# W2 block sums of a Strassen-like MLP computed on GpSimd instead of VectorE

## The chip, the cores and the metric

The kernel runs on one core of a Trainium2 chip. The metric is the device time of one execution in microseconds (us), as the median of several runs.

## What is computed

The reference is a two-layer streaming-encoder trunk on 512 frames of width 1024 in float32. Layer 0 mixes tokens by two gated linear recurrences, layer 1 by latent attention with rotary positions. Behind each mixer stands a squared-ReLU MLP of width 4096, and this case is about the MLPs:

```
def rope(x, cos, sin):
    ...
def sq_relu_mlp(h, w1, w2):
    return jnp.square(jax.nn.relu(h @ w1)) @ w2

def reference(x, positions, norm_gains, ..., mlp_w1, mlp_w2):
    for l in range(DEPTH):
        h = rmsnorm(x, norm_gains[l, 0])
        m = ...                                   # the layer's mixer
        x = x + rmsnorm(m, norm_gains[l, 1])
        h = rmsnorm(x, norm_gains[l, 2])
        x = x + rmsnorm(sq_relu_mlp(h, mlp_w1[l], mlp_w2[l]), norm_gains[l, 3])
    return x
```

## The kernel before

**Number format.** Each operand of a matrix product is split into a high and a low part, and three matmuls (`mm3`, L1827 to L1829: low by high, high by low, high by high) make one product. ScalarE casts the high part (`split_high`, L596 and L598; `operand`, L1072), then VectorE subtracts to get the low part (`split_low`, L605 without and L607 with a gain; `operand_low`, L1535). TensorE waits for the low part by the count `lo_ready` or `block_low`.

**The MLP.** The hidden width of 4096 is walked through in slices of 512. Six of them (SUBS = 6) are multiplied with W2 by a Winograd-Strassen scheme of seven products of half size instead of eight. For each slice s the scheme needs four blocks of W2 as they are (B11, B12, B21, B22, each 256 rows by 512 columns, held as 128 partitions by 1024 elements) and four sums of them, made in place in the buffers of the raw blocks: T1 = B12 - B11 in the buffer of B11, T2 = B22 - T1 in the buffer `spare`, T4 = B21 - T2 in the buffer of B21, T3 = B22 - B12 in the buffer of B12. Likewise four sums of blocks of the hidden values (S1 to S4). The raw blocks lie in `raw`. `spare` also holds, at another time of the step, the third of the four units of W1 (called w1_2 here; w1_0, w1_1 and w1_3 lie in `stage`). The four w1 units serve the up projection.

**One step.** `body(b)` is a step, b = 1 to 6 in each layer; steps 2 to 5 are one loop. Every engine has its own list in program order, and the lists meet in semaphores only. On TensorE a step is: up tile 0 (24 matmuls, w1_3 is needed at the 19th), products P1, P2, P1, P2 (first and second half of the tokens, six matmuls each), up tile 1, P5, P3, P5, P3, up tile 2, P7, P4, P7, up tile 3, P6, P4, P6. P5 uses T1, P7 uses T3, P4 uses T4 and P6 uses T2. Two banks of PSUM serve the up tiles and the products P1, P5, P7 and P6 in turn, so that a product or tile waits until the bank was read: up tiles by ScalarE (`up`, relu at L1064, square at L1066), products by VectorE (`gather`, L1550 in the first step and L1554 in the others). The second P1 waits for the relu of up tile 0, and that relu waits until VectorE has split S2, since it overwrites the buffer of S2. The second P5 waits for the relu of up tile 1, which stands in ScalarE's list behind the high parts of T1, T3 and T4.

**VectorE's list** in a step begins with the split of B21, the sum S4 (`hid_sum`, L1539) and the split of S2; then the four sums T1, T2, T4, T3 (`weight_sum`, L1543) stand between two gathers and the splits of T1, S4 and T3. At the step's end come the splits of B11, S3, w1_0 and w1_1, a gather, w1_2, the sums S1 and S2, and the splits of A12 and w1_3, all for the next step.

**GpSimd's list** has the pairwise differences of the gates (L788) in layer 0's mixer, later the rope angles (L807 to L819, a chain in which each instruction waits for the one before), a load of a gain, and four memsets for the attention mask (to L828). Behind them stand only DMA issues until the end.

**The DMA queue of SyncE** (`load_mlp`) loads the raw blocks of the next step: B11 when T1 was split (L704 and L681), B22 when the fourth sum is there, B12 when T3 was split, B21 when T4 was split, w1_3 when w1_0 was split.

The sums in VectorE's list, word for word:

```
weight_sum("T1", "B12", "B11", (stage_in[RAW_OF["B12"]], b12_loaded[layer, s] + 16 * i))
gather("P1", 0, 1, 1, s, i)
weight_sum("T2", "B22", "T1", (t_ready, made + 1))
gather("P1", 1, 0, 3, s, i)
low("T1", s, i)
weight_sum("T4", "B21", "T2", (t_ready, made + 2))
operand_low("S4", s, i)
weight_sum("T3", "B22", "B12", (t_ready, made + 3))
low("T3", s, i)
```

## Time and profile before

| what | value |
|---|---|
| median of 3 runs | 1232.18 us (1231.8 to 1235.79) |
| the profiled execution, its own time | 1229.68 us |
| its span in the profile | 1228.0 us |
| TensorE busy | 1174.5 us, 96% |
| VectorE busy | 816.6 us, 67% |
| ScalarE busy | 627.1 us, 51% |
| GpSimd busy | 114.6 us, 9% |
| mean granted clock of TensorE | 0.987 |

The profile is of one execution, and its time lies 2.5 us under the median. Its own time is 1.7 us more than its span, which is what lies before the first and behind the last instruction. PE is TensorE (PEld its weight loads), DVE is VectorE, ACT is ScalarE, POOL is GpSimd. Matmuls are pipelined: one of 512 columns is shown with 0.39 us, but the next begins 0.227 us behind it. Likewise a VectorE instruction's end overlaps the start of the next by about 0.08 us.

### The profile page before, as it was taken

The page shows a single profiled execution, that of the slowest core. Times are in us where ns is not written, and L with a number is a line of the kernel's source. Part 1 is how long each engine was busy: PE and PEld are TensorE (multiplying, and loading weights), DVE is VectorE, ACT ScalarE, POOL GpSimd, SP SyncE. Part 2 cuts the span into 40 slices and gives each one's busy share as a digit, 9 for nine tenths or more (in the row PEclk, how much of TensorE's full clock was granted, in tenths as well). Part 3 has the DMA queues.
Part 4 walks back from the last instruction along what each step waited for, and adds up shares of the span by engine and source line. Part 5 has one row for each costly group of instructions (what it writes and reads, how often), then busy time and mean ns, then how long its engine had stood idle before and what let it go on. Part 6 is the DMA issues. An engine that isn't in the chain of part 4 may idle for free.

```text
span 1228.0 us, 16266 instructions
## 1 busy us (share of the span) xinstructions
PE 1174.5 (96%) x5851; PEld 968.3 (79%) x5851; DVE 816.6 (67%) x1216; ACT 627.1 (51%) x1177; POOL 114.6 (9%) x129
## 2 busy tenths in 40 slices
PE   6999999999989999999899998999999999999897
PEld 5777788877968888888778776778978888888686
DVE  5566867875587687668556256865577677767644
ACT  5554555454645454545435675654655445545331
POOL 2331212310191000000000000100000000000000
PEclk9999899999999999999999999999999999999999
DMA  4322121133423332231222232212423332331221
GB/s 143 102 69 68 40 66 53 52 112 130 146 68 105 119 110 94 89 117 52 86 86 84 63 88 59 65 40 86 155 88 101 103 120 89 99 105 49 69 86 68
DMA packets 87490, 108.18 MB, mean 88 GB/s; under 512 B 9186, under 2 KB 48195, under 8 KB 87428
## 3 DMA queue, kind: packets, MB, share of 16 engines
q1 hardware_dynamic: 85684, 101.85, 26.1%
q0 software_dynamic: 1744, 5.51, 1.4%
q8 instruction: 38, 0.62, 0.2%
q14 instruction: 24, 0.20, 0.0%
HBM read 104.20 MB, written 2.10 MB: 87 GB/s over the span
## 4 chain that ended last, share of the span: by engine, by line
PE 79%; DVE 10%; ACT 7%; issue 2%; DMA 1%; POOL 0%; DVEq 0%; SPq 0%; ACTq 0%
PE bank L1827 21%; PE bank L1829 20%; PE bank L1828 20%; PE pp L1827 3%; PE pp L1828 3%; PE pp L1829 3%; PE pp L1969 2%; PE po L2308 1%; DVE y L1630 1%; DVE w_lo L607 1%; PE pp L1872 1%; DMA stage<-in_mlp_w 1%; ACT w_hi L598 1%; ACT w_hi L596 1%; PE pp L2289 1%
## 5 line engine op out<-in xcount | busy, mean ns | idle before, releaser
L1827 PE MATMUL bank<-h_lo,w_hi 128*128 128x512 f32 (+4 forms) x764 | 293.3, 384 | 12.0 <-DVE w_lo L607 5.9
L1829 PE MATMUL bank<-h_hi,w_hi 128*128 128x512 f32 (+4 forms) x764 | 289.8, 379 | 0.0
L1828 PE MATMUL bank<-h_hi,w_lo 128*128 128x512 f32 (+4 forms) x764 | 289.7, 379 | 0.0
L1827 PEld LDWEIGHTS bank<-h_lo,w_hi 128*128 128x128 f32 (+1 forms) x764 | 142.5, 187 | 43.3 <-DVE w_lo L607 7.5
L1829 PEld LDWEIGHTS bank<-h_hi,w_hi 128*128 128x128 f32 (+1 forms) x764 | 142.6, 187 | 27.3
L1828 PEld LDWEIGHTS bank<-h_hi,w_lo 128*128 128x128 f32 (+1 forms) x764 | 142.7, 187 | 25.4
L1827 PE MATMUL bank<-wx,a_hl 128*128 128x512 f32 x320 | 125.9, 393 | 0.5 <-ACT sq L1064 0.5
L1828 PE MATMUL bank<-wx,a_hl 128*128 128x512 f32 x320 | 125.0, 391 | 0.0
L1829 PE MATMUL bank<-wx,a_hl 128*128 128x512 f32 x320 | 125.0, 391 | 0.0
L596 ACT CAST wx<-raw 128x1024 fp32r<-128x1024 f32 x72 | 74.5, 1048 | 98.2 <-DVE raw L1543 67.0
L1554 DVE TENSOR_TENSOR y<-y,bank 128x512 f32<-128x512 f32 x80 | 54.8, 684 | 88.2 <-PE bank L1829 88.2
L605 DVE TENSOR_TENSOR wx<-raw,wx 128x1024 fp32r<-128x1024 f32 x72 | 88.7, 1232 | 30.0 <-ACT wx L596 29.7
L607 DVE SCALAR_TENSOR_TENSOR w_lo<-stage,vec,w_hi 128x512 fp32r<-128x512 f32 (+2 forms) x128 | 82.7, 697 | 21.0 <-ACT w_hi L598 21.0
L598 ACT ACTIVATE w_hi<-stage,vec 128x512 fp32r<-128x512 f32 (+2 forms) x128 | 78.4, 668 | 16.3 <-DMA stage<-in_mlp_w 15.8
L788 POOL TENSOR_TENSOR dec<-b_sb 128x512 f32<-128x512 f32 x48 | 58.1, 1222 | 185.3 <-DVE b_sb L1419 70.8
L605 DVE TENSOR_TENSOR w_lo<-stage,w_hi 128x1024 fp32r<-128x1024 f32 (+1 forms) x45 | 57.3, 1274 | 24.0 <-ACT w_hi L596 12.2
L1827 PEld LDWEIGHTS bank<-wx,a_hl 128*128 128x128 f32 x320 | 60.4, 189 | 13.2 <-ACT sq L1064 0.9
L1829 PEld LDWEIGHTS bank<-wx,a_hl 128*128 128x128 f32 x320 | 60.3, 189 | 12.7
L1828 PEld LDWEIGHTS bank<-wx,a_hl 128*128 128x128 f32 x320 | 60.4, 189 | 12.2
L596 ACT CAST w_hi<-stage 128x1024 fp32r<-128x1024 f32 (+1 forms) x45 | 46.0, 1025 | 11.5 <-DMA stage<-in_mlp_w 8.5
L1064 ACT ACTIVATE tmp<-bank 128x512 f32<-128x512 f32 x28 | 16.7, 598 | 65.5 <-PE bank L1829 65.3
L1827 PE MATMUL bank<-w_lo,a_hl 128*128 128x512 f32 x112 | 45.4, 406 | 3.0 <-DVE a_hl L1432 1.6
(362 smaller groups left out, 2175.6 us busy)
## 6 DMA issues: line engine op xcount, KB each, us to landing
stage<-in_mlp_w SPq DMA_DIRECT2D x68, 512.0 KB, 3.7
raw<-in_mlp_w SPq DMA_DIRECT2D x48, 512.0 KB, 3.5
stage<-in_ev_w_in SPq DMA_DIRECT2D x28, 512.0 KB, 3.8
spare<-in_mlp_w SPq DMA_DIRECT2D x12, 512.0 KB, 4.8
stage<-in_ev_w_out SPq DMA_DIRECT2D x8, 512.0 KB, 3.5
stage<-in_od_w_out SPq DMA_DIRECT2D x8, 512.0 KB, 3.5
stage<-in_od_w_in SPq DMA_DIRECT2D x10, 256.0 KB, 2.9
x_tok<-in_x SPq DMA_DIRECT2D x4, 512.0 KB, 5.3
```

What stands on the lines that cost most here:

```text
L596: ins = nc.scalar.copy(hi, src)
L598: ins = nc.scalar.activation(hi, src, ACT.Copy, scale=vec[:, g:g + 1])
L605: ins = nc.vector.tensor_tensor(lo, src, hi.bitcast(F32), ALU.subtract)
L607: ins = nc.vector.scalar_tensor_tensor(out=lo, in0=src, scalar=vec[:, g:g + 1], in1=hi.bitcast(F32), op0=ALU.mult, op1=ALU.subtract)
L788: nc.gpsimd.tensor_tensor(dec[:, item % 3, :].rearrange("p (b j) -> p b j", j=2 * L), b_sb[:, :].rearrange("p (b j) -> p b j", j=2 * L), r ...
L1064: nc.scalar.activation(f, banks[m][:, :], ACT.Relu).then_inc(up_read, 1)
L1554: nc.vector.tensor_tensor(dst, dst, banks[src][:, :], ALU.add).then_inc(prod_read, 1)
L1630: nc.vector.tensor_tensor(dst, a, b, ALU.add).then_inc(c_ready, 1)
L1827: nc.tensor.matmul(dst, wh, xl_, start=first, stop=False)
L1828: nc.tensor.matmul(dst, wl, xh, start=False, stop=False)
L1829: return nc.tensor.matmul(dst, wh, xh, start=False, stop=last)
L1969: ins = nc.tensor.matmul(dst[o], k_, q_, start=True, stop=True)
```

## The change

The four sums per step leave VectorE's list and stand in GpSimd's. Those of layer 0 stand behind the rope angles and the mask's memsets, those of layer 1 at the end of the list. GpSimd waits by name for what VectorE's order gave for free: T1 for the split of B11 and the load of B12, T2 for the split of w1_2 (whose buffer it overwrites), T4 for the split of B21. The order T1, T2, T4, T3 stays. The load of the next B11 now also waits for T2, which reads T1 out of that buffer.

```diff
@@ load_mlp, on SyncE
                     t_split("T1", 0, i)
+                    sp.wait_ge(t_ready, SUM_N * layer + 2 + 4 * i)
                     load_block("B11", 1, i)
@@ on GpSimd
+            def weight_sums(layer):
+                block_at = {b: buffers[RAW_OF[b]] for b in RAW_OF}
+
+                def weight_sum(what, a, b, after):
+                    pool.wait_ge(*after)
+                    nc.gpsimd.tensor_tensor(block_at[what], block_at[a], block_at[b], ALU.subtract).then_inc(t_ready, 1)
+
+                def is_split(u):
+                    pool.wait_ge(hi_ready, u + 1)
+                    pool.wait_ge(lo_ready, u + 1)
+
+                for sub in range(SUBS):
+                    made = SUM_N * layer + 4 * sub
+                    is_split(unit_no[("B11", layer, sub)])
+                    weight_sum("T1", "B12", "B11", (stage_in[RAW_OF["B12"]], b12_loaded[layer, sub]))
+                    is_split(unit_no[("w1", layer, sub + 1, 2)])
+                    weight_sum("T2", "B22", "T1", (t_ready, made + 1))
+                    is_split(unit_no[("B21", layer, sub)])
+                    weight_sum("T4", "B21", "T2", (t_ready, made + 2))
+                    weight_sum("T3", "B22", "B12", (t_ready, made + 3))
...
             nc.gpsimd.memset(mask_q[0:1, 0:P // 2].bitcast(F32), MASKED).then_inc(consts_ready, 1)
             nc.gpsimd.memset(mask_k[0:1, P // 2:P].bitcast(F32), 1.0).then_inc(consts_ready, 1)
+            weight_sums(0)
             pool.wait_ge(x_new[1], KD)
             load_gain(2)
...
             pool.wait_ge(x_new[2], KD)
             load_gain(3)
+            weight_sums(1)
@@ body of mlp, on VectorE
-                    weight_sum("T1", "B12", "B11", (stage_in[RAW_OF["B12"]], b12_loaded[layer, s] + 16 * i))
                     gather("P1", 0, 1, 1, s, i)
-                    weight_sum("T2", "B22", "T1", (t_ready, made + 1))
                     gather("P1", 1, 0, 3, s, i)
                     low("T1", s, i)
-                    weight_sum("T4", "B21", "T2", (t_ready, made + 2))
                     operand_low("S4", s, i)
-                    weight_sum("T3", "B22", "B12", (t_ready, made + 3))
                     low("T3", s, i)
```

VectorE's list in the first step of layer 0, before (here `wx<-raw,wx` are the splits of B21, T1 and T3, `tmp<-tmp,sq` is the sum S4, `a_hl<-sq,a_hl` the split of S2, `a_hl<-tmp,a_hl` that of S4, `y<-bank` a gather):

```order
L605 TENSOR_TENSOR wx<-raw,wx 128x1024 [waits hi_ready]
L1539 TENSOR_TENSOR tmp<-tmp,sq 128x2x256 [waits s_ready]
L1535 TENSOR_TENSOR a_hl<-sq,a_hl 128x512 [waits block_high]
L1543 TENSOR_TENSOR raw<-raw 128x1024 [waits stage_in3]
L1550 COPY y<-bank 128x512 [waits prod_done]
L1543 TENSOR_TENSOR spare<-raw 128x1024 [waits t_ready]
L1550 COPY y<-bank 128x512 [waits prod_done]
L605 TENSOR_TENSOR wx<-raw,wx 128x1024 [waits hi_ready]
L1543 TENSOR_TENSOR raw<-raw,spare 128x1024 [waits t_ready]
L1535 TENSOR_TENSOR a_hl<-tmp,a_hl 128x512 [waits block_high]
L1543 TENSOR_TENSOR raw<-raw 128x1024 [waits t_ready]
L605 TENSOR_TENSOR wx<-raw,wx 128x1024 [waits hi_ready]
```

Without the four rows of L1543 the list reads as below; nothing else of it has moved, and the lines' numbers are 22 higher because of the function added above them:

```order
L605 TENSOR_TENSOR wx<-raw,wx 128x1024 [waits hi_ready]
L1561 TENSOR_TENSOR tmp<-tmp,sq 128x2x256 [waits s_ready]
L1557 TENSOR_TENSOR a_hl<-sq,a_hl 128x512 [waits block_high]
L1567 COPY y<-bank 128x512 [waits prod_done] x2
L605 TENSOR_TENSOR wx<-raw,wx 128x1024 [waits hi_ready]
L1557 TENSOR_TENSOR a_hl<-tmp,a_hl 128x512 [waits block_high]
L605 TENSOR_TENSOR wx<-raw,wx 128x1024 [waits hi_ready]
```

GpSimd's list of the changed kernel, from the end of the rope angles into the first step's sums of layer 0 (L802 is the sum; T1, T2, T4, T3 in this order):

```order
L841 TENSOR_SCALAR cosd<-cosd 128x512 [waits pool_chain]
L795 DMA gbc<-in_norm_gains 128x1024 [waits sin_arg]
L847 MEMSET mask_q 128x128
L848 MEMSET mask_k 128x128 [waits pool_chain]
L849 MEMSET mask_q 1x64 [waits pool_chain]
L850 MEMSET mask_k 1x64
L802 TENSOR_TENSOR raw<-raw 128x1024 [waits stage_in3,lo_ready,hi_ready]
L802 TENSOR_TENSOR spare<-raw 128x1024 [waits t_ready,lo_ready,hi_ready]
L802 TENSOR_TENSOR raw<-raw,spare 128x1024 [waits t_ready,lo_ready,hi_ready]
L802 TENSOR_TENSOR raw<-raw 128x1024 [waits t_ready]
```

The sums now stand behind the whole angle chain, and a sum no longer waits for its place in VectorE's list: from the second step on it starts as soon as the named splits are done, T1 and T2 already at the end of the step before.

## Rows read from the trace of the kernel before

**Rows 1.** Busy time by stretch; columns: stretch, us, PE, PEld, DVE, ACT, POOL, PEclk, DMA.

```profile
440.00:480.00 40.00, 40.00 (x178) 33.14 (x177) 29.21 (x38) 20.81 (x30) 0.00 (x0) 1.00 0.31 104
...
356.00:360.00 4.00, 4.00 (x12) 3.10 (x12) 4.00 (x5) 0.14 (x1) 3.83 (x3) 0.59 0.72 251
```

**Rows 2.** Waits of TensorE over the whole span: total us, times, longest.

```profile
PE bank L1827 <- DVE tmp L1665: 12.0, 2, 6.0
```

**Rows 3.** The sums, line L1543: count, ns min/median/max, first and last start.

```profile
L1543 DVE TENSOR_TENSOR raw<-raw x24: 1212/1217/2304, 359.4 to 1119.8; 128x1024 f32<-128x1024 f32 x24
```

**Rows 4.** Time line, GpSimd, rope angles: start us, us, instruction.

```profile
342.09 1.30 POOL L817 TENSOR_TENSOR sind<-rinv,gbc 128x512 f32<-128x512 f32 x1
343.48 1.49 POOL L816 TENSOR_SCALAR gbc<-gbc 128x512 f32<-128x512 f32 x1
...
359.31 1.32 POOL L817 TENSOR_TENSOR cosd<-rinv,gbc 128x512 f32<-128x512 f32 x1
360.72 2.35 POOL L816 TENSOR_SCALAR gbc<-gbc 128x512 f32<-128x512 f32 x1
...
372.58 0.14 POOL L828 MEMSET mask_k<- 1x64 f32 x1
```

**Rows 5.** The same of VectorE beside them, first step of layer 0.

```profile
359.41 2.30 DVE L1543 TENSOR_TENSOR raw<-raw 128x1024 f32<-128x1024 f32 x1
...
367.15 1.80 DVE L1535 TENSOR_TENSOR a_hl<-tmp,a_hl 128x512 fp32r<-128x512 f32 x1
```

**Rows 6.** Line L788, two-input differences on GpSimd: count, ns min/median/max.

```profile
L788 POOL TENSOR_TENSOR dec<-b_sb x48: 1037/1154/2067, 43.6 to 251.5; 128x512 f32<-128x512 f32 x48
```

**Rows 7.** Time line of VectorE around the start of layer 0's second step.

```profile
386.80 1.23 DVE L605 TENSOR_TENSOR wx<-raw,wx 128x1024 fp32r<-128x1024 f32 x1 [0.39 <-ACT wx L596]
387.94 0.68 DVE L1535 TENSOR_TENSOR a_hl<-rinv,a_hl 128x512 fp32r<-128x512 f32 x1
388.56 2.74 DVE L607 SCALAR_TENSOR_TENSOR w_lo<-stage,vec,w_hi 128x512 fp32r<-128x512 f32 x4
392.51 0.69 DVE L1550 COPY y<-bank 128x512 f32<-128x512 f32 x1 [1.22 <-PE bank L1829]
393.12 1.41 DVE L607 SCALAR_TENSOR_TENSOR w_lo<-spare,vec,w_hi 128x512 fp32r<-128x512 f32 x2
394.44 0.68 DVE L1539 TENSOR_TENSOR sq<-sq,tmp 128x512 f32<-128x512 f32 x1
...
396.37 1.41 DVE L607 SCALAR_TENSOR_TENSOR w_lo<-stage,vec,w_hi 128x512 fp32r<-128x512 f32 x2
...
398.90 1.22 DVE L605 TENSOR_TENSOR wx<-raw,wx 128x1024 fp32r<-128x1024 f32 x1
...
400.64 0.68 DVE L1535 TENSOR_TENSOR a_hl<-sq,a_hl 128x512 fp32r<-128x512 f32 x1
...
423.88 0.69 DVE L1554 TENSOR_TENSOR y<-y,bank 128x512 f32<-128x512 f32 x1 [4.07 <-PE bank L1829]
```

**Rows 8.** Time line of TensorE: two places of a second step, three of first steps.

```profile
399.11 0.39 PE L1827 MATMUL bank<-h_lo,w_hi 128*128 128x512 f32 x1
...
403.19 0.39 PE L1827 MATMUL bank<-wx,a_hl 128*128 128x512 f32 x1
...
355.78 0.50 PE L1827 MATMUL bank<-h_lo,w_hi 128*128 128x512 f32 x1 [2.65 <-DVE w_lo L607]
...
373.14 0.50 PE L1827 MATMUL bank<-wx,a_hl 128*128 128x512 f32 x1 [0.51 <-ACT sq L1064]
...
906.55 0.50 PE L1827 MATMUL bank<-h_lo,w_hi 128*128 128x512 f32 x1 [2.17 <-DVE w_lo L607]
```

**Rows 9.** Time line of ScalarE: high parts of T3 and T4, and a relu.

```profile
370.60 2.00 ACT L596 CAST wx<-raw 128x1024 fp32r<-128x1024 f32 x2 [7.28 <-DVE raw L1543]
...
401.41 0.60 ACT L1064 ACTIVATE sq<-bank 128x512 f32<-128x512 f32 x1 [3.91 <-DVE a_hl L1535]
```

**Rows 10.** VectorE in layer 1's first step, ahead of the split of w1_3.

```profile
904.48 0.69 DVE L1535 TENSOR_TENSOR a_hl<-tmp,a_hl 128x512 fp32r<-128x512 f32 x1 [1.39 <-ACT a_hl L1072]
```

More of the change, by code:

```diff
@@ L1526, in mlp @@
                 banks = [bank[(n0 + m) % 2] for m in range(4)]
-                flat_block = {b: buffers[RAW_OF[b]] for b in RAW_OF}
                 def low(what, sub, i):
@@ L1539, in hid_sum @@
                     nc.vector.tensor_tensor(hid_block[what], hid_block[a], hid_block[b], op).then_inc(s_ready, 1)
-                def weight_sum(what, a, b, after):
-                    dve.wait_ge(*after)
-                    nc.vector.tensor_tensor(flat_block[what], flat_block[a], flat_block[b],
-                                            ALU.subtract).then_inc(t_ready, 1)
                 def gather(product, tt, src, count, s, i):
```

## The prediction

> **What bounds the kernel now.** I read the page's first part, then the busy time by stretch, then TensorE's waits, and last the time lines of one step. The first shows TensorE busy for 96% of the span and VectorE for 67% (the table of the profile before). The stretches say more: in a middle step TensorE is busy for all 40 of 40 us at the full clock, and VectorE for 29.2 [rows 1]. A step is 180 matmuls at 0.227 us, 40.8 us, and nothing but TensorE sets it. So the 4.6 us that four sums take from VectorE in a step (4 of 1.14 us from start to start; 1.217 us each by the median of their line [rows 3]) lie beside TensorE's work already. A gain could come only where TensorE waits for VectorE because of a sum. The largest such wait, twice 6.0 us at L1665 behind the last step of each MLP [rows 2], comes behind steps in which VectorE idles anyway (4.07 us ahead of one gather in every step [rows 7]), so a relief inside the step does not reach it. What is left is the question what the sums cost when GpSimd makes them.
>
> **What one sum costs on GpSimd.** The trace has no such instruction of 1024 elements. A two-input instruction of 512 elements takes 1.30 us while VectorE is idle [rows 4], and 1.15 us by the median of L788, where one input repeats one element [rows 6]. Twice 1.30 is 2.6, twice 1.04 (the shortest of L788) is 2.1; something like 0.15 us is spent once per instruction (a memset of 64 elements takes 0.14 [rows 4]), so I take 2.45 us, nearest to the row that has two true inputs, and keep 2.1 and 2.6 as ends. On VectorE it was 1.22.
>
> The Trainium skill (GPSIMD Engine Reference, Performance versus the Vector engine) gives 4497 ns for a two-input add of 2048 elements; half of that is 2.25 us, and by it the sum below would be some 6 us smaller.
>
> **What the two engines do to each other.** At 359.31 GpSimd starts a two-input instruction that ends at 360.63. VectorE's first sum starts 0.10 us later and takes 2.30 us instead of 1.22: it stands still until GpSimd is through and then takes its usual time [rows 4, 5]. The same at 367.15, 1.80 us for a split that takes 0.68 elsewhere [rows 5, 7]. And at 360.72 GpSimd takes 2.35 us for what it does in 1.49 with VectorE idle [rows 4]: it waits until the sum that runs is finished, but it is served before VectorE's next one. So one of the two engines holds something for a whole instruction when VectorE has two SBUF inputs, and they alternate. I put the hold of a 1024-element sum at 2.4 us.
>
> The Trainium skill (SBUF — State Buffer, Who interferes with whom) speaks against the change with the same picture: a port pair shared by the two engines, an exclusive lock, and the second one to issue blocks fully. If that page were wrong and these rows had another cause, the first rival below would hold.
>
> **The middle steps: walk through the one that begins at 395.03.** Every instruction of VectorE here except the gathers has two SBUF inputs.
> - The split of B11 (386.80) frees T1 on GpSimd at 388.0. VectorE is then splitting S3 (387.94) [rows 7]. T1 gets its turn at 388.55 and holds until 390.95. The four w1 pieces that began at 388.56 begin at 390.95, and w1_1 is done at 393.6 instead of 391.2. The idle 1.22 us ahead of the gather at 392.51 [rows 7] take up half of it: gather from 393.6, w1_2 until 395.55.
> - The split of w1_2 frees T2. VectorE runs S1 (before at 394.44 [rows 7], now 395.55 to 396.2), T2 holds 396.2 to 398.6. Then S2 and the split of A12 (0.6 us each) and w1_3 (two of 0.67), done at 401.15 where it was 397.7. TensorE needs it at 399.11 [rows 8]. **First stall 2.1 us.**
> - Behind that come a gather, the split of S1, the split of B21 (before at 398.90 [rows 7]) until 403.5, and S4. The split of B21 frees T4, which holds 404.1 to 406.5. The split of S2 (before at 400.64 [rows 7]) ends at 407.1, the relu of up tile 0 waits for just that (as it did at 401.41 [rows 9]) and ends at 407.8, and the second P1 waits for the relu. It began at 403.19 [rows 8]; with the first stall it would at 405.3. **Second stall 2.5 us.**
> - T3 holds 2.4 us while VectorE has two gathers; their banks are needed only by up tile 1, at 405.9 before and 410.5 now. Cost nothing. T1, T3, T4 and T2 are then there before they were, and their splits have the idle 4.07 us of [rows 7] behind them. B11, B22, B12 and B21 are loaded behind those splits with more than 15 us before use, and the new wait for T2 is long fulfilled when T1 is split. Cost nothing. The load of w1_3 comes 2.4 us later behind w1_0 and its cast too, but VectorE reaches its split later still.
>
> That is 4.6 us a step; with h for the hold it is about 3h - 2.6. Each MLP has five such steps (2 to 6): 10 x 4.6 = 46 us.
>
> **Layer 1, first step.** T1 finds VectorE idle. T2 holds 2.4 us behind S1, and 1.39 us of idleness stood there ahead of the split of A12 [rows 10]; TensorE already waits 2.17 us for w1_3 [rows 8], so the first stall grows by 0.9 at once. T4 comes as in the other steps and costs 2.0. **2.9 us.**
>
> **Layer 0, first step.** Here the sums stand behind the angles, and those end with the memset at 372.58 [rows 4], when T3 had already been made. Without four sums beside it GpSimd loses some 2 us less to VectorE (0.86 us at 360.72 alone [rows 4]), so T1 runs 370.8 to 373.2, T2 to 375.7. VectorE splits T1 behind T2 (until 376.8), T4 holds until 379.2, S4's split until 379.8, T3 until 382.3. ScalarE casts T3 and T4 in 2.0 us as before [rows 9], and the relu of up tile 1 ends at 384.9. The second P5 waits for it, and began at 373.14 [rows 8]. **11.8 us.** TensorE stands still for 7 us of these; a stretch near half clock followed the stall of 2.65 us at 355.78 [rows 8] (12 matmuls in 4 us and a granted clock of 0.59 from 356 to 360 [rows 1]), six matmuls lost, 1.4 us. I add one such: **1.4 us.** GpSimd's later work (gain loads, rotary halves) waits for x or for VectorE, not for its own list: nothing.
>
> **The sum.** 46 + 2.9 + 11.8 + 1.4 = 62 us. The profiled execution took 1229.7, so 1292 by it; it lies 2.5 us under the median of the runs, and on that I predict 1294. The hold between 2.05 and 2.6 us moves ten steps by -1.0 and +0.6 each: 1283 to 1301.
>
> **Rivals.**
> - *The port costs VectorE nothing.* If VectorE's instructions go first and GpSimd takes the gaps, the middle steps stay at 40.8 us, because all four sums are needed 10 us or more later. Left are 11.8 + 1.4: **1245**. Against it stand the two stretched rows [rows 5]; for it, that no 1024-element sum on GpSimd has been seen. 12%.
> - *Only one stall per step.* If T4's wait for the split ends over 0.6 us late, the split of S2 goes ahead of T4, and the second stall is gone: 62 - 11 x 2.3 gives **1269**. GpSimd would need 0.6 us to notice a semaphore. 10%.
> - *The clock falls in every step.* Two stalls of over 2 us stand within 9 us, and the one of 2.65 us at 355.78 was followed by a stretch near half clock [rows 1, 8]. With 1.4 us for each of 11 steps: **1309**. Against it: the stall of 2.17 us at 906.55 [rows 8] was followed by none. 10%.
> - *Faster.* If VectorE carries a backlog from the sums of step 6 into the chain at L1665, TensorE's 12.0 us of waits there [rows 2] shrink by up to four sums per layer, 2 x 4.6 us: **1223**, provided that GpSimd's hold costs nothing and the angles are done in time. It decides only if VectorE has no idle time behind T3; it has 4.07 us and more in each step [rows 7]. 2%.
> - *No change.* The sums' lateness in layer 0's first step would have to vanish too, for instance if the angle chain without VectorE's sums beside it ended 9 us earlier. 2%.
>
> **How the numbers follow.** Forecast 64%. The predicted time is the forecast's. 1260 to 1311 holds it, the single stall and the clock case: 84%. The first rival lies outside. A measurement of this kernel can tell some 0.3% (4 us) from no change: faster 2%, within 0.3% 2%, slower 96%.
>
> **What the profile of the changed kernel would show.** Right: 48 sums on POOL of about 2.4 us; TensorE under 37 of 40 us in a middle step, with stalls behind the split of w1_3 (VectorE, L607) and behind the relu (ScalarE) before the second P1; VectorE splits of 512 elements that take some 3 us; a gap near 370 in layer 0 that ends with ScalarE's relu near 385. Wrong: middle steps of 40.8 us, or sums on POOL that are stretched themselves to 3 us and more while VectorE's are not.

## The result and the profile after

| | before | after |
|---|---|---|
| median of 3 runs | 1232.18 us (1231.8 to 1235.79) | 1264.21 us (1263.87 to 1266.02) |
| the profiled execution, its own time | 1229.68 us | 1266.02 us |
| its span | 1228.0 us | 1264.3 us |
| TensorE busy | 1174.5 us, 96% | 1186.7 us, 94% |
| VectorE busy | 816.6 us, 67% | 822.0 us, 65% |
| GpSimd busy | 114.6 us, 9% | 245.7 us, 19% |
| mean granted clock | 0.987 | 0.982 |

The ratio is 1.0258, with a 95% interval of 1.0231 to 1.0285: 32 us slower. The forecast was 1294 us, 62 us slower. The direction and the range held, but the likeliest case did not: half of the loss it names is not there. The time is near that of the rival "only one stall per step" (1269).

VectorE gave 48 sums of 1.2 us away, some 58 us, and yet its busy time rose by 5 us. What it had saved is in its record again as time in which it stood still behind GpSimd. Busy time by stretch, the same 40 us as in [rows 1] (columns as there), and the 4 us behind layer 1's first stall:

```profile
440.00:480.00 40.00, 38.52 (x170) 31.38 (x169) 29.94 (x33) 19.44 (x29) 11.21 (x4) 1.00 0.32 105
```

```profile
932.00:936.00 4.00, 4.00 (x12) 3.11 (x11) 2.58 (x4) 1.30 (x3) 2.49 (x1) 0.57 0.75 260
```

TensorE was busy for 40.00 of 40 us there; now it is for 38.52, where the forecast wanted less than 37. The four sums are GpSimd's 11.21 us. The sums by form (count, ns min/median/max, first and last start), in place of [rows 3]:

```profile
L802 POOL TENSOR_TENSOR raw<-raw x24: 2336/2402/2747, 368.1 to 1152.4; 128x1024 f32<-128x1024 f32 x24
L802 POOL TENSOR_TENSOR spare<-raw x12: 2348/2732/2740, 370.6 to 1141.3; 128x1024 f32<-128x1024 f32 x12
L802 POOL TENSOR_TENSOR raw<-raw,spare x12: 3134/3336/3358, 373.1 to 1149.0; 128x1024 f32<-128x1024 f32 x12
```

A sum that does not have to wait takes 2.34 to 2.40 us (T3, in the first row; so do the first two of layer 0). T1 and T2 show 2.73, and T4, in the third row, 3.34. What is above 2.4 is taken as waiting for VectorE: 0.35 us for T1 and T2, 0.94 for T4. The forecast expected stretched rows on VectorE alone, and had named sums of 3 us and more as a sign that it was wrong. T4's 0.94 us is the first sign of what it had wrong.

TensorE's waits, as in [rows 2] (total us, times, longest):

```profile
PE bank L1840 <- DVE w_lo L607: 21.9, 14, 3.1
PE bank L1840 <- DVE tmp L1678: 12.0, 2, 6.0
```

The wait for w1_3 (VectorE's `w_lo`) was 5.9 us in 3 places and is now 21.9 us in 14. The wait of 12.0 us behind the last step of each MLP is what it was. The steps themselves, from up tile 0 to the next up tile 0: a middle step took 40.80 us and takes 42.72, in both layers.

| part of the span | before | after | difference |
|---|---|---|---|
| start to up tile 1 of layer 0's first step | 364.31 | 362.92 | -1.4 |
| from there to up tile 0 of the second step | 30.72 | 42.23 | +11.5 |
| from there to up tile 1 of layer 0's sixth step | 174.08 | 183.83 | +9.8 |
| from there to up tile 1 of layer 1's first step | 344.38 | 351.28 | +6.9 |
| from there to up tile 1 of layer 1's sixth step | 203.99 | 213.38 | +9.4 |
| from there to the end of the span | 110.5 | 110.6 | +0.2 |

The fourth row is not the change's alone: the same stretch took from 344.4 to 350.9 us in the executions profiled for this study whose steps were undisturbed. Of its 6.9 us, 4.7 lie ahead of the first matmul of layer 1's MLP and 2.2 between that and up tile 1 of its first step. The medians differ by 32 us, the two profiled executions by 36.

**One middle step, on VectorE, GpSimd, ScalarE and TensorE.** It is the step of [rows 7]; everything lies later by 10 us because of the first step. VectorE (start us, us, instruction):

```profile
398.67 4.88 DVE L607 SCALAR_TENSOR_TENSOR w_lo<-stage,vec,w_hi 128x512 fp32r<-128x512 f32 x4
...
406.11 2.79 DVE L1561 TENSOR_TENSOR sq<-sq 128x512 f32<-128x512 f32 x1
408.82 0.68 DVE L1557 TENSOR_TENSOR a_hl<-tmp,a_hl 128x512 fp32r<-128x512 f32 x1
409.43 1.40 DVE L607 SCALAR_TENSOR_TENSOR w_lo<-stage,vec,w_hi 128x512 fp32r<-128x512 f32 x2
410.75 0.68 DVE L1567 COPY y<-bank 128x512 f32<-128x512 f32 x1
...
411.95 1.21 DVE L605 TENSOR_TENSOR wx<-raw,wx 128x1024 fp32r<-128x1024 f32 x1
413.09 0.68 DVE L1561 TENSOR_TENSOR tmp<-tmp,sq 128x512 f32<-128x512 f32 x1
413.69 0.68 DVE L1557 TENSOR_TENSOR a_hl<-sq,a_hl 128x512 fp32r<-128x512 f32 x1
414.29 0.67 DVE L1571 TENSOR_TENSOR y<-y,bank 128x512 f32<-128x512 f32 x1
```

GpSimd, the four sums T1, T2, T4, T3:

```profile
398.27 2.74 POOL L802 TENSOR_TENSOR raw<-raw 128x1024 f32<-128x1024 f32 x1 [19.28 <-DVE wx L605]
405.61 2.74 POOL L802 TENSOR_TENSOR spare<-raw 128x1024 f32<-128x1024 f32 x1 [4.59 <-DVE w_lo L607]
413.30 3.34 POOL L802 TENSOR_TENSOR raw<-raw,spare 128x1024 f32<-128x1024 f32 x1 [4.95 <-DVE wx L605]
416.71 2.39 POOL L802 TENSOR_TENSOR raw<-raw 128x1024 f32<-128x1024 f32 x1
```

ScalarE's relu of up tile 0:

```profile
414.46 0.60 ACT L1088 ACTIVATE sq<-bank 128x512 f32<-128x512 f32 x1 [4.71 <-DVE a_hl L1557]
```

TensorE, the matmul that needs w1_3 and the first of the second P1:

```profile
410.88 0.50 PE L1840 MATMUL bank<-h_lo,w_hi 128*128 128x512 f32 x1 [1.49 <-DVE w_lo L607]
...
415.13 0.47 PE L1840 MATMUL bank<-wx,a_hl 128*128 128x512 f32 x1
```

T1 holds back the four w1 pieces (4.88 us instead of 2.74) and T2 the sum S2 (2.79 instead of 0.69). With that w1_3 is split late, and TensorE's matmul at 410.88 starts 1.88 us behind the one before it (409.00), where 0.23 is usual. That is 1.65 us; slower starts of the matmuls behind the wait make up the rest of the 1.92 that the step has lost. That is the forecast's first stall. Then T4 asks at 413.30, while S4 is being summed. The forecast let it in next, ahead of the split of S2. It was not: the split of S2 follows S4 at once (413.69, 0.68 us), T4 gets its turn only behind it, the relu comes at 414.46, and the second P1 begins without a stall, though with nothing to spare: the relu ends at 415.06, and the matmul starts at 415.13. VectorE's gather at 414.29 takes its usual 0.67 us beside T4: one of its operands lies in PSUM.

**Layer 0's first step.** GpSimd, from the end of the angle chain on (in place of the last row of [rows 4]):

```profile
367.95 0.14 POOL L850 MEMSET mask_k<- 1x64 f32 x1
368.06 2.34 POOL L802 TENSOR_TENSOR raw<-raw 128x1024 f32<-128x1024 f32 x1
370.57 2.35 POOL L802 TENSOR_TENSOR spare<-raw 128x1024 f32<-128x1024 f32 x1 [0.17 <-POOL raw L802]
373.08 3.13 POOL L802 TENSOR_TENSOR raw<-raw,spare 128x1024 f32<-128x1024 f32 x1 [0.17 <-POOL spare L802]
376.30 2.70 POOL L802 TENSOR_TENSOR raw<-raw 128x1024 f32<-128x1024 f32 x1
```

VectorE beside it, the splits of T1 and S4 (the second was 1.80 us in [rows 5]):

```profile
371.51 2.49 DVE L605 TENSOR_TENSOR wx<-raw,wx 128x1024 fp32r<-128x1024 f32 x1 [9.05 <-ACT wx L596]
373.92 2.85 DVE L1557 TENSOR_TENSOR a_hl<-tmp,a_hl 128x512 fp32r<-128x512 f32 x1
```

ScalarE, in place of [rows 9], and TensorE behind both of its stalls:

```profile
379.08 1.99 ACT L596 CAST wx<-raw 128x1024 fp32r<-128x1024 f32 x2 [7.09 <-POOL raw L802]
380.98 0.59 ACT L1088 ACTIVATE sq<-bank 128x512 f32<-128x512 f32 x1
```

```profile
374.10 0.77 PE L1840 MATMUL bank<-wx,a_hl 128*128 128x512 f32 x1 [5.57 <-issue]
...
381.62 0.50 PE L1840 MATMUL bank<-wx,a_hl 128*128 128x512 f32 x1 [1.88 <-ACT sq L1088]
```

Here the forecast held nearly row for row: T1 and T2, the split of T1 behind T2, T4 ahead of the split of S4, T3, two casts, relu, second P5. Only the angle chain ended 4.6 us earlier than before (2 us were expected; 1.4 us of the 4.6 is that the whole step began earlier in this execution), and the larger stall, of 5.6 us, sits ahead of the first P5, which needs the split T1.

### The profile page after: what moved, and what is told of

Same layout as the page of the kernel before. It is cut to its first block, busy times and chain, and to the rows that moved or that the text cites. A ratio compares the mean times of both kernels' runs of the same rounds, so it can differ in the third digit from the quotient of the medians.

```text
span 1264.3 us, 16278 instructions
## 1 busy us (share of the span) xinstructions
PE 1186.7 (94%) x5851; PEld 970.9 (77%) x5851; DVE 822.0 (65%) x1168; ACT 627.8 (50%) x1177; POOL 245.7 (19%) x177
## 4 chain that ended last, share of the span: by engine, by line
PE 64%; DVE 15%; ACT 8%; issue 7%; POOL 4%; DMA 2%; DVEq 0%; SPq 0%; ACTq 0%; POOLq 0%
PE bank L1840 17%; PE bank L1841 16%; PE bank L1842 16%; DVE w_lo L607 4%; PE pp L1841 2%; PE pp L1842 2%; PE pp L1840 2%; PE po L2321 1%; DVE y L1643 1%; PE pp L1982 1%; ACT wx L596 1%; DVE sq L1561 1%; PE pp L1885 1%; DVE a_hl L1557 1%; DMA stage<-in_mlp_w 1%
## 5 line engine op out<-in xcount | busy, mean ns | idle before, releaser
L1840 PE MATMUL bank<-h_lo,w_hi 128*128 128x512 f32 (+4 forms) x764 | 295.3, 387 | 27.8 <-DVE w_lo L607 21.9
L1840 PEld LDWEIGHTS bank<-h_lo,w_hi 128*128 128x128 f32 (+1 forms) x764 | 143.0, 187 | 63.0 <-DVE w_lo L607 27.8
L1840 PE MATMUL bank<-wx,a_hl 128*128 128x512 f32 x320 | 128.1, 400 | 9.0 <-issue 5.6
L1842 PE MATMUL bank<-wx,a_hl 128*128 128x512 f32 x320 | 126.1, 394 | 0.0
L1841 PE MATMUL bank<-wx,a_hl 128*128 128x512 f32 x320 | 126.1, 394 | 0.0
L605 DVE TENSOR_TENSOR wx<-raw,wx 128x1024 fp32r<-128x1024 f32 x72 | 104.6, 1452 | 28.4 <-ACT wx L596 28.1
L607 DVE SCALAR_TENSOR_TENSOR w_lo<-stage,vec,w_hi 128x512 fp32r<-128x512 f32 (+2 forms) x128 | 104.5, 866 | 19.3 <-ACT w_hi L598 19.3
L802 POOL TENSOR_TENSOR raw<-raw 128x1024 f32<-128x1024 f32 x24 | 61.2, 2549 | 230.7 <-DVE wx L605 229.7
L1088 ACT ACTIVATE sq<-bank 128x512 f32<-128x512 f32 x28 | 16.7, 598 | 90.2 <-DVE a_hl L1557 55.0
L596 ACT CAST w_hi<-stage 128x1024 fp32r<-128x1024 f32 (+1 forms) x45 | 46.0, 1024 | 11.9 <-DMA stage<-in_mlp_w 8.6
```

The lines of the kernel that those rows point to most:

```text
L596: ins = nc.scalar.copy(hi, src)
L605: ins = nc.vector.tensor_tensor(lo, src, hi.bitcast(F32), ALU.subtract)
L607: ins = nc.vector.scalar_tensor_tensor(out=lo, in0=src, scalar=vec[:, g:g + 1], in1=hi.bitcast(F32), op0=ALU.mult, op1=ALU.subtract)
L802: nc.gpsimd.tensor_tensor(block_at[what], block_at[a], block_at[b], ALU.subtract).then_inc(t_ready, 1)
L1088: nc.scalar.activation(f, banks[m][:, :], ACT.Relu).then_inc(up_read, 1)
L1840: nc.tensor.matmul(dst, wh, xl_, start=first, stop=False)
```

## The experiments

Three questions were open: does each part of the loss come from where the time lines put it, what decides whether T4 goes ahead of the split of S2, and does any placement of the sums on GpSimd beat the kernel before. Kernels are named by what is edited. Where a kernel was run once only, its time is compared with the median of the kernel before on the same chip, and the reading rests on its time lines. Ratios and their 95% intervals are worked out from all runs of a comparison and can differ a little from the quotient of the two medians.

**1. Layer 0's sums on VectorE as before (T2, T4 and T3 at their old places too), layer 1's on GpSimd.**

```diff
             nc.gpsimd.memset(mask_k[0:1, P // 2:P].bitcast(F32), 1.0).then_inc(consts_ready, 1)
-            weight_sums(0)
...
+                    on_dve = layer == 0
+                    if on_dve:
+                        weight_sum("T1", "B12", "B11", (stage_in[RAW_OF["B12"]], b12_loaded[layer, s] + 16 * i))
...
```

> Layer 0's sums back on VectorE, layer 1's on GpSimd as in the change. Theory P (a port that one engine holds for a whole instruction): layer 1 pays 1.9 us in each of its five middle steps and some 2 in its first, so about 1243 to 1245 us, and its steps last 42.7 us while those of layer 0 last 40.8. Rival L (the cost is mostly lateness behind the rope angles in layer 0): about 1234, steps of 40.8 in both layers.

Measured: 1241.44 us, ratio 1.0101 (1.0074 to 1.0128), 12.4 us over the 1229.07 of the kernel before. Middle steps take 40.80 us in layer 0 and 42.7 in layer 1. The loss per step belongs to the steps whose sums GpSimd makes, and layer 0 carries the rest, some 20 us.

**2. T4 asked for a little earlier.** GpSimd waits for the low part of a block only, one semaphore instead of two.

```diff
                 def is_split(u):
-                    pool.wait_ge(hi_ready, u + 1)
                     pool.wait_ge(lo_ready, u + 1)
```

> GpSimd waits for lo_ready alone ahead of T1, T2 and T4, not for hi_ready and lo_ready, so that each sum is asked for a little earlier (the low part implies the high one). T4 then comes earlier into VectorE's sum S4. If the split of S2 went ahead of T4 by a close race in time, T4 now goes first, the second P1 stalls by some 2.4 us, a middle step lasts about 45 us and the time is near 1288. If the order does not hang on the moment of asking, steps stay at 42.7 us and the time at 1264.

Measured: 1260.56 us, ratio 1.0256 (1.0228 to 1.0284), as the change itself. T4 stood at GpSimd 0.44 us before the split of S2 began instead of 0.39, took 3.39 us, and still came behind it. 0.05 us decide nothing; the edit moves the moment by no more.

**3. T1 asked for only behind the split of S2.** One wait more, so that all four sums stand where VectorE has gathers to do and TensorE has its P1 and P2.

```diff
                     is_split(unit_no[("B11", layer, sub)])
+                    pool.wait_ge(block_low["S2"], SUBS * layer + sub + 1)
                     weight_sum("T1", "B12", "B11", (stage_in[RAW_OF["B12"]], b12_loaded[layer, sub]))
```

> T1 on GpSimd also waits until VectorE has split S2, so that no sum runs beside the splits of w1 at the end of a step. Theory P: the stall ahead of w1_3 is gone, middle steps last 40.8 us, and only layer 0's first step stays late: about 1243 us. Rival W (the stall has another cause, such as the later load of w1_3 or more DMA traffic): middle steps stay near 42.7 us and the time near 1264.

Measured: 1260.12 us, ratio 1.0259 (1.0230 to 1.0288). Neither side had it. The stall at w1_3 is gone from every middle step (10.88 us from up tile 0 to up tile 1, as before), so the hold by T1 and T2 was its cause. But a new wait took its place: the four sums now follow each other, and ScalarE casts T3 and T4 ahead of the relu of up tile 1, for which the second P5 waits. GpSimd, ScalarE and TensorE in one middle step:

```profile
464.93 2.72 POOL L802 TENSOR_TENSOR raw<-raw 128x1024 f32<-128x1024 f32 x1
```

```profile
467.74 2.00 ACT L596 CAST wx<-raw 128x1024 fp32r<-128x1024 f32 x2 [7.19 <-POOL raw L802]
469.64 0.59 ACT L1089 ACTIVATE sq<-bank 128x512 f32<-128x512 f32 x1
```

```profile
470.28 0.50 PE L1841 MATMUL bank<-wx,a_hl 128*128 128x512 f32 x1 [1.14 <-ACT sq L1089]
```

T3 is there at 467.65, the casts end at 469.74, and the second P5 begins 1.3 us late: 42.24 us a step.

**4. The wait of 3, and the sums of layer 0's first step ahead of the rope angles.**

```diff
+            weight_sums(0, range(1))
             ch.link(nc.gpsimd.tensor_copy(angle, pos_i))
...
-            weight_sums(0)
+            weight_sums(0, range(1, SUBS))
```

> As e3, and the four sums of layer 0's first step stand ahead of the rope angles. Theory P: no stall by sums anywhere; and since the angles no longer run beside the first step's splits of w1, TensorE's stalls of 1.0 and 2.7 us and the stretch at half clock there go too: about 1227 to 1230 us, 2 to 5 less than before the change. Rival: the angles, now some 30 us later, hold VectorE up in the second step instead, and T1 of the second step comes late behind them: 1236 or more.

Measured: 1249.95 us, ratio 1.0171 (1.0144 to 1.0199). The first step is clean, 30.27 us where the change has 42.23. But the angles, put off by four sums, run into the second step beside its own sums and VectorE's w1 splits, and that step takes 49.5 us (four stalls of 1.1 to 2.7 us); the others take 42.24. Work of some 33 us on GpSimd that shares something with VectorE costs wherever it meets a step: moved from one, it costs in the next.

**5. The wait of 3, and ScalarE's relu of up tile 1 ahead of the casts of T3 and T4.** VectorE's split of T3 moves behind that of A22 to match.

```diff
@@ body of mlp, on ScalarE
-                    weights("T3", s, i, done + 3)
-                    weights("T4", s, i, done + 4)
                     up(1, b, i)
...
                     operand("A22", (up_hid, hids), done - 1)
+                    weights("T3", s, i, done + 3)
+                    weights("T4", s, i, done + 4)
```

> As e3, and ScalarE does the relu of up tile 1 (with A11 and A22 behind it) ahead of the casts of T3 and T4; VectorE splits T3 behind A22. Theory P with the chain seen in e3 (four sums one behind the other end 11 us after the split of S2, and the relu stands behind their casts): the 1.5 us stall ahead of the second P5 goes, middle steps last 40.8 us in both layers, and what is left is layer 0's first step, some 8 to 12 us: 1238 to 1243. Rival (GpSimd's four sums in a row are too late for TensorE whatever the order): steps of 41.5 us or more, 1250 and above.

Measured: 1239.61 us, ratio 1.0071 (1.0049 to 1.0092). Every middle step takes 40.8 us again. What is left is layer 0's first step: 40.54 us instead of 30.72, with 7.9 us on TensorE from one matmul's start to the next ahead of 373.76 (a wait of 7.5) and 10.2 us at half clock around and behind it.

**6. The same, but layer 0's first step's sums on VectorE as before.** GpSimd makes the other 44.

```diff
-            weight_sums(0)
+            weight_sums(0, range(1, SUBS))
...
+                    on_dve = layer == 0 and s == 0
+                    if on_dve:
+                        weight_sum("T1", "B12", "B11", (stage_in[RAW_OF["B12"]], b12_loaded[layer, s] + 16 * i))
...
```

> The version with the gate and the relu first (ratio 1.0071), but in layer 0's first step the four sums stand in VectorE's list as before; GpSimd makes the other 44. Theory: all that this version still lost was the lateness of that one step (40.5 us where before had 30.7). Then every middle step takes 40.8 us, the first step 30.7, and the time is that of before within 0.3%, no gain either, since TensorE is the bound in every step. Rival: the sums of step 2 now stand beside VectorE's work of a step that begins earlier, or the order of ScalarE's casts costs something in the first steps: then 0.5 to 1% slower.

Measured over 12 runs against 17 of the kernel before: 1228.83 us against 1233.43, ratio 0.9977 (0.9958 to 0.9995). This is as good as the kernel before; if it is better, then by a quarter of a per cent, within what a measurement of this kernel can tell from no change. Its middle step has VectorE at 27.8 of 40 us instead of 29.2, and that buys nothing:

```profile
440.00:480.00 40.00, 40.00 (x178) 33.12 (x177) 27.83 (x35) 20.80 (x30) 10.70 (x4) 1.00 0.31 102
```

TensorE is busy for all 40 us in both. The one gain that the time line of its MLP steps shows is 0.8 us in layer 0's first: the wait of 0.5 us ahead of the second P5 [rows 8] is gone, and ScalarE's relu of up tile 1 now stands ahead of the casts of T3 and T4. That reordering could be made without GpSimd; it was not tried alone.

**7. Half sums.** To size the hold: each sum covers 512 of its 1024 elements.

```diff
-                    nc.gpsimd.tensor_tensor(block_at[what], block_at[a], block_at[b], ALU.subtract).then_inc(t_ready, 1)
+                    nc.gpsimd.tensor_tensor(block_at[what][:, 0:1, :], block_at[a][:, 0:1, :], block_at[b][:, 0:1, :],
+                                            ALU.subtract).then_inc(t_ready, 1)
```

> The change's kernel, but each sum covers only the first 512 of the 1024 elements of a block; the other half of the sums is left out. A sum takes 1.3 us and holds 1.2. Theory P: the two holds ahead of the split of w1_3 cost VectorE 2.4 us instead of 4.7, less than the idle time and the margin there together, so no stall: middle steps 40.8 us, and layer 0's first step shorter by some 4 us: near 1240. Rival F (a fixed cost for each sum or each wait, not its length): steps stay near 42.7 us.

Measured: 1237.87 us in one run, 5 us over the kernel before. The sums take 1.30 us (medians 1300, 1626 and 2229 ns for the three forms), middle steps 40.9 us, layer 0's first step 37.6. With a hold of half the length, the slack of the step covers nearly all of it.

**8. The kernel before, with the angles put off.** They start only when the first step's four sums are made (on VectorE). Does the port cost anything in the kernel before?

```diff
+            pool.wait_ge(t_ready, 4)
             pool.dma_start(pos_i, positions.partition_broadcast(P)).then_inc(pos_in, 16)
```

> The kernel before the change, sums on VectorE, but GpSimd starts the rope angles only when the four sums of layer 0's first step are made. Theory P: the first step loses the stalls of 1.0, 2.65 and 0.5 us and the stretch at half clock, some 5 us; in the second and third step the angles' short holds lie within VectorE's margins: about 4 us less than before, 1225 to 1229. Rival: the angles make the split of w1_3 or a gather late in the later steps, and the time stays at that of before or above.

Measured: 1232.24 us against 1232.74, ratio 1.0002 (0.9983 to 1.0021). From one matmul's start to the next, the gaps around the start of the first step shrank (one of 2.7 us instead of 1.4 and 3.1, and the 0.9 us later are gone), but the second step became 4.45 us longer by three stalls, where the angles now run:

```profile
396.10 0.50 PE L1828 MATMUL bank<-h_lo,w_hi 128*128 128x512 f32 x1 [0.99 <-DVE w_lo L607]
399.91 0.50 PE L1828 MATMUL pp<-wx,a_hl 128*128 128x512 f32 x1 [0.79 <-DVE wx L605]
...
403.32 0.50 PE L1828 MATMUL bank<-wx,a_hl 128*128 128x512 f32 x1 [1.76 <-ACT sq L1065]
```

So GpSimd's angles cost this kernel a few us already before the change, and a later place only moves the bill.

**9. The split of S2 in another form.** Now the step of the forecast that failed, T4 ahead of the split of S2. VectorE's split of S2 becomes a `scalar_tensor_tensor` with a factor of one read from memory, the form of the w1 splits, of the same size.

```diff
-                    nc.vector.tensor_tensor(lo, hid_block[what], hi.bitcast(F32), ALU.subtract).then_inc(block_low[what], 1)
+                    if what == "S2":
+                        nc.vector.scalar_tensor_tensor(out=lo, in0=hid_block[what], scalar=ones[:, 0:1], in1=hi.bitcast(F32),
+                                                       op0=ALU.mult, op1=ALU.subtract).then_inc(block_low[what], 1)
+                    else:
+                        nc.vector.tensor_tensor(lo, hid_block[what], hi.bitcast(F32),
+                                                ALU.subtract).then_inc(block_low[what], 1)
```

> In the change's kernel the split of S2 is issued as a scalar_tensor_tensor with a factor of one out of memory, the kind that GpSimd's T1 was served ahead of. Theory K (whether a waiting sum goes ahead hangs on the kind of VectorE's next instruction): T4 now holds ahead of the split of S2, that split takes about 2.9 us, the second P1 stalls by some 2.4 us, a middle step lasts about 45 us and the time is near 1287. Rival M (it hangs on something else, such as the moment of asking or the pair of instructions): split of S2 0.74 us, steps 42.7 us, time near 1263.

Measured: 1289.69 us in one run, 57 over the kernel before, and close to the forecast's 62. VectorE, GpSimd and TensorE in one middle step:

```profile
455.73 2.87 DVE L1558 SCALAR_TENSOR_TENSOR a_hl<-sq,ones,a_hl 128x512 fp32r<-128x512 f32 x1
```

```profile
455.33 2.71 POOL L802 TENSOR_TENSOR raw<-raw,spare 128x1024 f32<-128x1024 f32 x1 [4.95 <-DVE wx L605]
```

```profile
459.33 0.50 PE L1845 MATMUL bank<-wx,a_hl 128*128 128x512 f32 x1 [2.04 <-ACT sq L1088]
```

T4 asks 0.40 us before the split would begin, as in the changed kernel, and now goes ahead of it. The split takes 2.87 us, and the second P1 starts 2.4 us behind the matmul before it, 2.2 more than usual. A step lasts 44.9 us.

**10. A memset of one element per partition between S4 and the split of S2.** It tells whether it was the operand read as a scalar.

```diff
                     hid_sum("S4", "A12", "S2", ALU.subtract, (s_ready, made + 3))
+                    nc.vector.memset(scrap[:, :], 0.0)
                     operand_low("S2", s, i)
```

> The changed kernel with one instruction more in VectorE's list: a memset of one element per partition, which reads nothing, between the sum S4 and the split of S2. Theory A, GpSimd's waiting sum gets in only where VectorE's two-input instructions do not follow each other directly: T4 goes ahead of the split of S2, that split takes 2.8 us, the second stall of 2.5 us per step appears as with the scalar_tensor_tensor, and the time is near 1288. Theory B, it was the operand read as a per-partition scalar in that instruction that let GpSimd in: T4 stays behind the split of S2, takes 3.3 us, and the time stays near 1262.

Measured: 1298.52 us in one run, 65 over the kernel before. The memset takes 0.06 us and opens the door to a sum of 2.4:

```profile
459.33 2.85 DVE L1558 TENSOR_TENSOR a_hl<-sq,a_hl 128x512 fp32r<-128x512 f32 x1
459.34 0.06 DVE L1584 MEMSET scrap<- 128x1 f32 x1
```

```profile
458.93 2.71 POOL L803 TENSOR_TENSOR raw<-raw,spare 128x1024 f32<-128x1024 f32 x1 [4.94 <-DVE wx L606]
```

The split itself is the plain form again, so theory A's order holds here. The time is ten us above A's 1288. Four of the stretches of 3.4 us at half clock fell into steps with two stalls, some 1.5 us lost each, but so did four in experiment 9. The 8.8 us between the two profiles lie all over the span (1.8 ahead of the first step's up tile 1, 2.9 between the MLPs), one run stands for each, and the difference is not explained. The third rival of the forecast wanted such a stretch in every step.

**11. The split of S2 in two plain pieces, of 448 and 64 elements.** It tells length of waiting from direct succession.

```diff
-                    operand_low("S2", s, i)
...
+                    for a, z in ((0, 224), (224, 256)):
+                        lo, full, hi = [v[:, :, a:z] for v in parts]
+                        ins = nc.vector.tensor_tensor(lo, full, hi, ALU.subtract)
+                    ins.then_inc(block_low["S2"], 1)
```

> The changed kernel with the split of S2 cut into two plain two-input instructions, the first over 448 of the 512 elements, the second over the last 64; both follow the sum S4 directly. In the changed kernel T4 asks 0.39 us before the split of S2 begins and lets it go ahead. Here it asks 0.39 us before the first piece and about 0.9 us before the second. Theory C, what counts is how long GpSimd has been waiting when VectorE's next instruction comes up (0.83 us before was enough in layer 0's first step): T4 goes between the two pieces, the second piece takes some 2.5 us, and with a second stall of 2.4 us per step the time is 1285 to 1300. Theory D, VectorE keeps what it holds as long as plain two-input instructions follow each other directly: both pieces go ahead of T4, T4 takes 3.4 us, and the time is 1262 to 1266.

Measured: 1269.17 us in one run, 34 over the kernel before in its one run there; middle steps 42.8 us. T4 waits through both pieces, as theory D has it for this place, and theory C falls.

```profile
456.93 0.68 DVE L1561 TENSOR_TENSOR tmp<-tmp,sq 128x512 f32<-128x512 f32 x1
457.54 0.74 DVE L1588 TENSOR_TENSOR a_hl<-sq,a_hl 128x448 fp32r<-128x448 f32 x2
```

```profile
457.14 3.40 POOL L802 TENSOR_TENSOR raw<-raw,spare 128x1024 f32<-128x1024 f32 x1 [4.95 <-DVE wx L605]
```

Theory D is right for this place in the list and not in general. In every step of experiments 3 to 5, T4 was let in between the plain splits of T1 and S4, which follow each other directly, just as in layer 0's first step of the changed kernel (371.51 and 373.92 above); it asks 0.83 us before the split of S4 there. Nor does VectorE give way because it has just been made to wait itself. In experiment 4's first step the split of T1 took its usual 1.22 us, and the split of S4 was held back all the same:

```profile
357.57 1.22 DVE L605 TENSOR_TENSOR wx<-raw,wx 128x1024 fp32r<-128x1024 f32 x1
358.71 2.88 DVE L1559 TENSOR_TENSOR a_hl<-tmp,a_hl 128x512 fp32r<-128x512 f32 x1
```

```profile
357.87 3.17 POOL L802 TENSOR_TENSOR raw<-raw,spare 128x1024 f32<-128x1024 f32 x1 [0.17 <-POOL spare L802]
```

The kernel before has the same in layer 0's mixer. A two-input instruction of GpSimd (L788) asks some 0.18 us before a plain two-input instruction of VectorE that follows another directly. In 21 of 22 such places it was let in, and the second of the two took 1.3 us instead of 0.4:

```profile
52.76 0.42 DVE L1368 TENSOR_TENSOR xl<-k_sb,dec 128x256 f32<-128x256 f32 x1
53.10 1.31 DVE L1370 TENSOR_TENSOR xl<-q_sb,dec 128x256 f32<-128x256 f32 x1
```

```profile
52.92 1.21 POOL L788 TENSOR_TENSOR dec<-b_sb 128x512 f32<-128x512 f32 x1 [5.19 <-DVE xl L1370]
```

So the form and directness of VectorE's next instruction can turn the order (experiments 9 and 10), but they are not the whole rule. The moment of asking is not excluded: 0.39 to 0.44 us ahead was passed over in the middle steps, 0.18 and 0.83 us ahead was let in at other places, and no run moved T4 by more than 0.05 us against the same pair of instructions. What decides stays open.

## Why the prediction was right and wrong

- **What bounds the kernel** held. In a middle step TensorE sets the time; taking 1.4 us net per step off VectorE in experiment 6 gained nothing there. The 12.0 us behind the last steps did not move.
- **The price of a sum**, 2.45 us, measured 2.34 to 2.40, so the forecast was a little high. The estimate of 2.25 us, half of the 4497 ns that the Trainium skill (GPSIMD Engine Reference, Performance versus the Vector engine) gives for 2048 elements, was a little low.
- **The exclusion of VectorE by GpSimd** held: 2.1 us for a hold of 2.4 in both rows where a sum was let in (4.88 and 2.79). The first rival, that the port costs nothing, falls by this and by experiments 3 and 7. The Trainium skill (SBUF — State Buffer, Who interferes with whom) describes an exclusive lock, with the second one to issue blocked fully. The rows agree with the lock: one engine waits until the other is through. They do not agree that the order of issue decides: T4 asked 0.39 us ahead of the split of S2 and was passed over, and in experiment 9 it asked as early and went first, where only the form of the split was another.
- **First stall, 2.1 us per step:** measured 1.9 (42.72 less 40.80), ten times, 1.65 of it the stall itself. Experiment 3 took T1 and T2 away from w1_3, and it vanished.
- **Second stall, 2.5 us per step: this step failed.** The forecast said "The split of B21 frees T4, which holds 404.1 to 406.5. The split of S2 ends at 407.1". It rested on the row at 360.72, where GpSimd was "served before VectorE's next one", and made that into a rule: they alternate. That row cannot show an order. VectorE's next instruction there was a gather, with one operand in PSUM, which ran at its usual speed beside GpSimd, and so did the sum behind it:

```profile
361.64 0.68 DVE L1550 COPY y<-bank 128x512 f32<-128x512 f32 x1
362.24 1.21 DVE L1543 TENSOR_TENSOR spare<-raw 128x1024 f32<-128x1024 f32 x1
```

  Other rows of the kernel before, the 21 of L788 above, would have supported the rule, and in the middle steps it failed nevertheless: T4 waited behind S4 and behind the split of S2, in all of them. The stall's own size was nearly right: where experiments 9 and 10 let T4 in, the second P1 started 2.2 us late in each step, and the totals were 57 and 65 us, stretches at half clock among them. So of the 30 us between forecast and result, ten steps of 2.5 and layer 1's first of 2.0 are 27; the first stall's 0.2 us a step are 2 more, and the rest is in the first steps, below. The rule was right for layer 0's first step, and there by luck as much as by insight, since what decides was not known.
- **The rival "only one stall per step"** came out at 1269, 5 us from the result, for a reason that it did not have. It asked for T4 to come over 0.6 us late. T4 asked 0.39 us ahead of the split, in time, and was passed over all the same.
- **Layer 1's first step, 2.9 us:** the second part was missing as above. TensorE waits 2.78 us for w1_3 where it waited 2.17 (0.9 more expected, 0.6 found):

```profile
931.69 0.50 PE L1840 MATMUL bank<-h_lo,w_hi 128*128 128x512 f32 x1 [2.78 <-DVE w_lo L607]
```

  A stretch at a granted clock of 0.57 followed (the row from 932), some 1.4 us that the forecast had excluded for this place by the row at 906.55.
- **Layer 0's first step, 11.8 us and 1.4 for the clock:** measured 11.5 in all, 1.7 less. The chain of causes was right. Counted from up tile 1, the second P5 began 9.9 us later than before instead of 11.8: T1 began 1.4 us earlier within the step than forecast (368.06 instead of 370.8, less the 1.4 us by which the step itself was early), and the sums went a little faster. Behind the second P5 another 1.6 us were lost, with a stretch of 3.4 us at half clock from 382.9, where 1.4 was counted. A longer stretch, 6.8 us from 372.7, cost nothing more: the first P5 ran in it, and TensorE then waited 1.88 us for the relu anyway.
- **Loads and the new wait of the B11 load** cost nothing, as stated: no wait of VectorE, ScalarE or TensorE in a middle step ended with one of the raw blocks' transfers. ScalarE's cast of w1_3 does wait longer for its transfer, and VectorE's split of it comes later still, as stated.

## What to carry to other kernels

Moving work from an engine with a third of its time free to an idle one gains nothing while a third engine sets the step, and it costs if the two share a resource: here 58 us of VectorE's work gone, and its busy time higher. Where two engines exclude each other, walk through the step and ask of each meeting who is second and what waits behind it; a row that shows one order at one place doesn't give the order at another, and both orders should be priced, since here they differ by nearly a factor of two in the total (57 us in experiment 9 against 32). If such work must be moved, put it where the other engine has PSUM operands or nothing to do, look at what the later place makes late (here ScalarE's casts ahead of a relu), and leave out the one step in which the receiving engine is still busy with something else.

## What was not expected of the hardware

- Which engine goes first when GpSimd asks during a two-input instruction of VectorE is neither plain alternation nor the order of asking. Between the sum S4 and the split of S2, a waiting GpSimd sum was passed over in every middle step, through one split or through two pieces of it (experiment 11). An instruction of 0.06 us that reads nothing, put between them, let the sum in (experiment 10), and so did another form of the same size, `scalar_tensor_tensor` (experiment 9). Between the splits of T1 and S4 the sum was let in although both are plain and follow directly. T2 got in between the sums S1 and S2, of which the second waits on a semaphore for the first (406.11). So one tiny instruction on VectorE, or its form, was worth 2.2 us a step here, and the rule behind it is not known.
- VectorE instructions with one operand in PSUM run beside a GpSimd sum at their usual speed, as the forecast had assumed: the gathers at 410.75 and 414.29 take 0.67 to 0.68 us.
- In the angle chain, `tensor_scalar` on GpSimd took 1.50 us for 512 elements with one arithmetic operation and 0.61 us with two (L840 at 364.19 and L841 at 365.77 of the changed kernel). Why is not known.
- Long stalls of TensorE came with longer stretches at half clock than was counted: with waits of 5.6 and 7.5 us (layer 0's first step here and in experiment 5) went stretches of 6.8 and 10.2 us at half clock, with the wait of 2.65 us in the kernel before [rows 8] one of 3.4 us. In layer 1's first step half clock followed a wait of 2.39 us in experiment 6, and none the one of 2.17 us in the kernel before. The waits of 1.5 us for w1_3 in the changed kernel's middle steps were followed by none.
